# Moving the key shift, the second scan's output and the score visits in a hybrid block kernel on one Trainium2 core

## What is computed

```python
h = rmsnorm(x, norm_w);  p = h @ w_in
r, k, v, g, dw, da = split(token_shift(pa, mu))        # branch 1
kk = k * k_k;  kh = kk / max(norm_per_head(kk), 1e-12)
def step(s, inp):                                       # per head, 64 x 64 state
    sa = einsum('bhvk,bhk->bhv', s, kh_t)
    s = s * w_t - sa[..., None] * b_t + v_t[..., None] * k_t
    return s, einsum('bhvk,bhk->bhv', s, r_t)
oa = (layer_norm_per_head(y) * ln_w + ln_b + bonus) * silu(g)
ob = rmsnorm((ssd_chunked(silu(conv4(xbc))) + d_skip * xs) * silu(z))   # branch 2
oc = bg * conv3(cg * xin) * silu(g3)                                    # branch 3
merged = sum_n sigmoid(gate_n) * (o_n @ w_branch[n]);  out = rmsnorm(x + merged @ w_out)
```

## Time and profile before

| | |
|---|---|
| median of 3 runs (lowest, highest) | 1231.09 us (1230.35, 1233.09) |
| profiled execution: its time, its span | 1228.37 us, 1226.7 us |
| mean granted TensorE clock | 0.989 |
| TensorE matmuls busy | 1179.1 us, 96% |
| VectorE busy | 803.7 us, 66% |
| ScalarE busy | 574.2 us, 47% |
| GpSimd busy | 69.9 us, 6% |
| HBM traffic over the span | 160 GB/s |

### The profile page before, as it was taken

The page is one execution under the profiler, slowest core; times in us unless marked ns, Lnnn a source line. Parts: engine busy times, 40 slices in busy tenths (PEclk is TensorE's granted clock), DMA queues, the critical chain, the costliest instruction groups (busy, mean ns, idle before and its releaser), DMA issues.

```text
span 1226.7 us, 23555 instructions
## 1 busy us (share of the span) xinstructions
PE 1179.1 (96%) x8502; PEld 1047.3 (85%) x8502; DVE 803.7 (66%) x1174; ACT 574.2 (47%) x828; POOL 69.9 (6%) x94
## 2 busy tenths in 40 slices
PE   6998999999999999999999999999999999999996
PEld 5997989989889899899898988888888888888885
DVE  4786768688577686876867857564555555546553
ACT  5454445454354463544444544544444344444443
POOL 2001001010010010100101003000000000000000
PEclk9998999999999999999999999999999999999998
DMA  5755645546455354463553545566666656667662
GB/s 165 207 155 137 165 119 138 140 113 162 125 137 150 103 154 133 136 163 109 138 150 103 140 148 171 172 206 193 195 191 197 193 190 193 193 188 273 199 192 98
DMA packets 254747, 197.24 MB, mean 161 GB/s; under 512 B 23943, under 2 KB 207472, under 8 KB 254064
## 3 DMA queue, kind: packets, MB, share of 16 engines
q1 hardware_dynamic: 252228, 195.82, 55.0%
q10 hardware_dynamic: 2476, 0.84, 0.3%
HBM read 193.71 MB, written 2.11 MB: 160 GB/s over the span
## 4 chain that ended last, share of the span: by engine, by line
PE 91%; DVE 4%; ACT 1%; DMA 1%; issue 1%; POOL 1%; DVEq 0%; SPq 0%; ACTq 0%
PE ps L1158 14%; PE ps L1159 13%; PE ps L1160 13%; PE ps L1236 11%; PE ps L1237 11%; PE ps L1238 11%; PE ps L1484 2%; PE ps L1485 2%; PE ps L1486 2%; DVE wlo L721 1%; DVE lots L1040 1%; PE ps L1270 1%; ACT whi L427 1%; PE ps L1353 1%; PE ps L1345 1%
## 5 line engine op out<-in xcount | busy, mean ns | idle before, releaser
L721 DVE TENSOR_TENSOR wlo<-raw,whi 128x1024 fp32r<-128x1024 f32 (+1 forms) x356 | 439.8, 1247 | 239.4 <-ACT whi L427 237.9
L427 ACT ACTIVATE whi<-raw 128x1024 fp32r<-128x1024 f32 (+1 forms) x356 | 373.4, 1054 | 316.8 <-PE ps L1238 181.2
L1158 PE MATMUL ps<-hhi,whi 128*128 128x256 f32 (+1 forms) x1440 | 424.9, 295 | 0.2 <-DVE wlo L721 0.2
L1159 PE MATMUL ps<-hlo,whi 128*128 128x256 f32 (+1 forms) x1440 | 409.8, 285 | 0.0
L1160 PE MATMUL ps<-hhi,wlo 128*128 128x256 f32 (+1 forms) x1440 | 409.4, 284 | 0.0
L1158 PEld LDWEIGHTS ps<-hhi,whi 128*128 128x128 f32 (+1 forms) x1440 | 276.9, 192 | 17.3 <-issue 13.8
L1159 PEld LDWEIGHTS ps<-hlo,whi 128*128 128x128 f32 (+1 forms) x1440 | 277.4, 193 | 0.7
L1160 PEld LDWEIGHTS ps<-hhi,wlo 128*128 128x128 f32 (+1 forms) x1440 | 276.9, 192 | 0.3
L1236 PE MATMUL ps<-whi,hhi 128*128 128x512 f32 x384 | 151.3, 394 | 0.0
L1238 PE MATMUL ps<-whi,hlo 128*128 128x512 f32 x384 | 149.6, 390 | 0.0
L1237 PE MATMUL ps<-wlo,hhi 128*128 128x512 f32 x384 | 149.5, 389 | 0.0
(11 more groups left out here) (270 smaller groups left out, 1140.6 us busy)
## 6 DMA issues: line engine op xcount, KB each, us to landing
raw<-in_w_in SPq DMA_DIRECT2D x548, 256.0 KB, 3.1
raw<-in_w_branch SPq DMA_DIRECT2D x96, 256.0 KB, 3.6
raw<-in_w_out SPq DMA_DIRECT2D x64, 256.0 KB, 3.6
o<-in_x SPq DMA_DIRECT2D x4, 1024.0 KB, 6.7
acb<-acs_rows SPq DMA_DIRECT2D x8, 256.0 KB, 3.5
out_y<-lots SPq DMA_DIRECT2D x3, 512.0 KB, 4.6
lots<-in_final_norm_w SPq DMA_DIRECT2D x1, 1024.0 KB, 10.3
lots<-ad SPq DMA_DIRECT2D x32, 8.0 KB
```

The lines of the kernel that those rows point to most:

```text
L427: sc.activation(whi[:, slot, :, 0:width], raw[:, slot, :, 0:width], ACT.Copy).then_inc(hi_done, 1)
L721: tt(wlo[:, slot, :, 0:width], raw[:, slot, :, 0:width], whi[:, slot, :, 0:width].bitcast(F32), ALU.subtract).then_inc(lo_done, 1)
L1158: mm(dst, a, khi, start=first, stop=False)
L1159: mm(dst, a, klo, start=False, stop=False)
```

## The change

Three groups of moves. In the scheme of slots, `V_P1` goes from 17 to 16, and with it everything that is counted from it; `V_XT` and `V_YB` go to 18 and 20, in front of the transition matrices, and their matmuls write bank C in place of E; the convolution and its tanh go with them (visits 14 and 16), and the masked inverse is made at visit 15. TensorE gets one more wait before the transition matrices, for the reader of bank C. Scores and transposes go one slot ahead on TensorE (3, 5, 7 to 2, 4, 6) and on the other engines (4, 6 to 3, 5; the copy at visit 9 to 7); the DMAs of the inverse that ScalarE sends go from visit 15 to 14, while the inverse itself stays at visits 9 to 12. On VectorE the layer norm is cut in two: reciprocal and first product, then `shift_rk` of the next round, then the last three operations at visit 33. The low splits at two visits of the scan go behind the state operations. The queue of SyncE is not edited.

```diff
 ORDER = (1, 0, 2, 3)
-V_P1 = 17
-V_XT = 25
-V_YB = 27
+V_P1 = 16
+V_XT = 18
+V_YB = 20
...
 
+            def shift_tile(j, a, t, bank, strip):
...
+                w = ORDER[2 * a + t]
+                proj(strip, t, bank + t, pq[:, w, 1:1 + T])
+                sc.activation(qq[:, w, :], ps[:, bank + t, 0:T], ACT.Copy,
+                              scale=omm[:, bass.ds(j + w * CT, 1)]).then_inc(tile_out, 1)
...
             def shift_pair(j, a, bank, strip):
...
                 for t in range(2):
-                    w = ORDER[2 * a + t]
-                    proj(strip, t, bank + t, pq[:, w, 1:1 + T])
-                    sc.activation(qq[:, w, :], ps[:, bank + t, 0:T], ACT.Copy,
-                                  scale=omm[:, bass.ds(j + w * CT, 1)]).then_inc(tile_out, 1)
+                    shift_tile(j, a, t, bank, strip)
...
                         sc.activation(s2g, sh[:, 3, :], ACT.Tanh, scale=0.5).then_inc(s["g_th"], 1)
-                    if t == 4:
+                    if t == 3:
...
                         sc.activation(seg, seg, ACT.Exp, scale=-1.0).then_inc(s["seg_e"], 1)
-                    if t == 9:
+                    if t == 7:
...
                         act.wait_ge(s["x_tr2"], j + 1)
-                        sc.activation(xst.rearrange("p b n -> p (b n)"), E[:, 0:T], ACT.Copy,
+                        sc.activation(xst.rearrange("p b n -> p (b n)"), C[:, 0:T], ACT.Copy,
...
                         proj(strip0 + 1, 1, BANKS[1] + 1, scb[:, 1, :]).then_inc(tile_out, 1)
-                    if t == 15:
+                    if t == 14:
...
                             act.dma_start(tb[:, q, :, :], sol_2[8 * q:8 * q + 8, :, :, :]).then_inc(s["t_in"], 16)
+                    if t == 16:
+                        act.wait_ge(s["x_s"], j * 4 + 4)
+                        sc.activation(cvt, cv, ACT.Tanh, scale=0.5).then_inc(s["x_th"], 1)
...
                         sc.activation(yy, A, ACT.Copy).then_inc(s["yx_ok"], 1)
-                        act.wait_ge(s["x_s"], j * 4 + 4)
-                        sc.activation(cvt, cv, ACT.Tanh, scale=0.5).then_inc(s["x_th"], 1)
...
                         sc.activation(yz.rearrange("p q n -> p (q n)"), A, ACT.Copy).then_inc(s["yz_ok"], 1)
-                    if t == 32:
+                    if t == 29:
...
                         sc.activation(ys, B[:, 0:T], ACT.Copy).then_inc(s["ys_ok"], 1)
-                    if t == 32 and not last:
-                        shift_pair(j + 1, 0, BANKS[3], strip0 + 3)
+                    if t in (31, 32) and not last:
+                        shift_tile(j + 1, 0, t - 31, BANKS[3], strip0 + 3)
...
                 for t in range(2 * (LAST + GATES) if last else SLOTS):
-                    if t % 2 == 0 and t // 2 < nchunks and t != V_ST + 2:
+                    if t % 2 == 0 and t // 2 < nchunks and t not in (V_ST + 1, V_ST + 3):
...
                         stt(s2g, s2g, 1.0, sh[:, 3, :], ALU.add, ALU.mult)
-                    if t == 4:
+                    if t == 3:
                         scores(0)
-                    if t == 6:
+                    if t == 5:
                         scores(1)
-                    if t == 17:
+                    if t == V_P1 - 1:
...
                         op.then_inc(s["state_ok"], 1)
-                    if t == V_ST + 2 and t // 2 < nchunks:
+                    if t in (V_ST + 1, V_ST + 3) and t // 2 < nchunks:
                         split_lo(base + t // 2 + AHEAD, (t // 2 + AHEAD) % RING)
-                    if t == 33:
+                    if t == 30:
...
                         v.tensor_copy(sol_l, sol_t.rearrange("p s t -> p t s")).then_inc(s["sol_tr"], 1)
-                    if t == 19:
+                    if t == 14:
...
                         conv4(s["x_s"], j * 4, j)
-                    if t == 21:
+                    if t == V_P1 + 3:
...
                         seg_times(1, 1).then_inc(s["seg_g"], 1)
-                    if t == 22:
+                    if t == V_XT - 1:
...
                         dve.wait_ge(s["yb_mm"], j + 1)
-                        stt(cv, xs2, dskh[:, bass.ds(j, 1)], E[:, T:2 * T], ALU.mult, ALU.add).then_inc(s["ob_d"], 1)
+                        stt(cv, xs2, dskh[:, bass.ds(j, 1)], C[:, T:2 * T], ALU.mult, ALU.add).then_inc(s["ob_d"], 1)
...
                         stt(yc, C[:, 0:T], -1.0 / 64, ys, ALU.mult, ALU.add).then_inc(s["yc_ok"], 1)
-                    if t == 29:
+                    if t == 27:
...
                             op.then_inc(s["sc_s"], 1)
-                    if t == 30:
+                    if t == 28:
...
                         tt(yo, yc, rin, ALU.mult).then_inc(s["ln_v"], 1)
+                    if t == 32 and not last:
+                        shift_rk(j + 1)
+                    if t == 33:
...
                             ).then_inc(s["oa_ok"], 1)
-                    if t == 33 and not last:
-                        shift_rk(j + 1)
...
                         norm_and_logits(j + 1)
-                    if t == 3:
+                    if t == 2:
...
                         op.then_inc(s["tr_vk"], 1)
-                    if t == 5:
+                    if t == 4:
...
                         score(1)
-                    if t == 7:
+                    if t == 6:
...
 
+                        pe.wait_ge(s["ob_d"], j + 1)
...
                         pe.wait_ge(s["xs_ok"], j + 1)
-                        pe.wait_ge(s["nm_ok"], j * 2 + 2)
+                        pe.wait_ge(s["vt_ok"], j + 1)
                         for b in range(2):
-                            op = tr(E[:, b * P:b * P + P], xs2[:, b * P:b * P + P], ident[:])
+                            op = tr(C[:, b * P:b * P + P], xs2[:, b * P:b * P + P], ident[:])
...
                             h = slice(64 * e, 64 * e + 64)
-                            mm(E[h, T:2 * T], xst[:, 0, h], seg[:, e, 0:T], start=True, stop=False, skip_group_check=True)
-                            op = mm(E[h, T + P:2 * T], xst[:, 1, h], seg[:, e, T:384], start=False, stop=True,
+                            mm(C[h, T:2 * T], xst[:, 0, h], seg[:, e, 0:T], start=True, stop=False, skip_group_check=True)
+                            op = mm(C[h, T + P:2 * T], xst[:, 1, h], seg[:, e, T:384], start=False, stop=True,
```

## The result

| | before | after |
|---|---|---|
| median (lowest, highest), 4 runs each | 1230.72 (1228.54, 1233.09) | 1250.17 (1249.10, 1251.49) |
| profiled execution, its span | 1228.37, 1226.7 | 1250.56, 1248.8 |
| mean granted clock | 0.989 | 0.983 |

The ratio is 1.0158, with a 95% interval of 1.0137 to 1.0180, so the loss is 19.5 us where 9.4 were forecast. The direction was right. The median lies just above the top of the stated range, 1250.0, and the size was off by a factor of two. The two profiled executions lie 22.2 us apart, since that of the kernel before is 2.4 us under its median. Lines behind the edits have new numbers in the code after: 1207, 1287 and 1315 are 1212, 1292 and 1320 there, 945 is 949, 721 is 725.

The account below looks back on a forecast made before the run. Bound by TensorE's matmuls with one hole a round: new losses 24.4 + 2.4 + 1.4 + 7 x 0.1 + 6.5 = 35.4 less 26.0 won gave +9.4 on 1231.1, so 1240.5 us. Its own range was 1234 to 1249, the overall one 1225 to 1250.

Parts of the forecast that it names:

- new wait for the inverse: TensorE at line 1315 waits for the masked inverse, 3.05 us in each of eight rounds: 24.4 us lost.
- hole at the turn: TensorE's wait at the key norm, line 1207, between rounds shrinks from 2.9 to 0.1 us in seven rounds.
- wait for the scaled keys: TensorE at line 1287 waits 0.35 us in seven rounds, 2.4 us, plus 1.4 us in the first round.
- clock, by the length of rounds: Half clock at the turns goes, winning 5.7 us; half clock behind the waits at line 1315 costs 6.5 us.
- Clock behind the new waits: Half clock follows the waits at line 1315 at the turns' rate: 8 x 4/7 x 1.42 = 6.5 us, bounds 0 and 11.4.
- rival of a solve that SyncE doesn't hold: Diagonals go out once reduced, ScalarE alone holds the solve: wait 1.95 us at line 1315, time 1224.5; chance 0.17.
- a turn with 1.4 us: Wait of 1.4 us stays between rounds because ScalarE reaches the sqrt late: 9.8 us more, 1250; chance 0.13.

Follow-up runs that it names:

- e3_sp: Changed kernel with both halves of the score diagonals sent ahead of chunk 9's load in SyncE's queue: 1235.64 us, 1.0046 of the kernel before.
- e4_scores: Changed kernel with scores and transposes back at their old slots and visits, the rest of the change kept: 1215.52 us, 0.9873 of the kernel before.
- e5_conv: Changed kernel with the four convolution taps at visit 15, behind the masked inverse instead of ahead of it: 1249.44 us, 1.0148 of the kernel before.
- e9_scores_only: Kernel before with only the transposes and scores moved one slot ahead, with their visits on VectorE and ScalarE: 1256.68 us, 1.0188 of the kernel before.
- e7_turn: Changed kernel with scores at the old slots and the key shift behind the whole layer norm again: 1234.42 us, 1.0033 of the kernel before.
- e8_best: Changed kernel with scores at old slots, diagonals ahead of chunk 9's load, and the short convolution's high part behind the sqrt: 1203.22 us, 0.9778 of before.
- e6_pad: Changed kernel with the two transposes of line 1427 made five times over, 0.9 us more TensorE work a round: 1252.27 us.
- e2_before: The kernel before, run once more without any edit, for the clock: 1228.96 us.

## Why the prediction was wrong in size

Point by point, by its own steps, in the profiled executions:

| step | forecast | measured |
|---|---|---|
| new wait for the inverse, eight rounds | +24.4 | +22.2 |
| hole at the turn | -20.3 + 0.7 | -16.1 |
| wait for the scaled keys | +3.8 | +5.0 |
| clock, by the length of rounds | -5.7 + 6.5 = +0.8 | -5.7 + 12.5 = +6.8 |
| matmuls busy for longer, not assigned | none | +4.3 |
| sum | +9.4 | +22.2 (the span: +22.1) |

- **The new wait** was right in place, cause and size. e3_sp shows SyncE's share, e4_scores that the moved scores and transposes bring it, e5_conv that taps and DMAs end together; e9_scores_only brings the wait forth in the old kernel.
- **The turn** was right in mechanism. The forecast 0.1 was 0.59, since the product of line 1039 took 0.4 us longer beside GpSimd's. The prediction didn't see that the new order lays it there. e7_turn prices the moved shift. e8_best closes the hole though that product is as long as before: its copy, load and low half are out of the way, and the load is over 1.36 us before the sqrt.
- **The scaled keys:** 0.35 forecast, 0.41 measured, in each of seven rounds. The first round's was 2.5 in this execution and 1.7 in the other; the forecast 1.4 came on top of the 0.3 that it had before.
- **The step that failed is "Clock behind the new waits".** It took the rate of the turns, 4 of 7, at 1.42 us each: 6.5 us. Measured: 8 of 8, one of them double, 12.5 us by the length of rounds. The price of 1.42 held; the rate didn't, and the prediction had no double stretches. That term was mis-sized by 6.0 us, the largest part of the 12.7 between forecast and measured span; the 4.3 that are not assigned and the turn's 3.5 come next. Its stated bound, 11.4 for eight of eight, came near, but the sum went by the rate. I took the rate of one execution for a chance per hole. e6_pad shows nearly equal holes met three times, spared four times and met once more, and e2_before other turns in the same kernel, so a rate counted in one execution is neither a property of the hole nor safely carried to another schedule. That this rate came from an execution 2.4 us under the median makes it a low one besides.

The loss between the medians is 2.7 us less than between the profiled executions. The prediction added its forecast for the fast profiled execution to the median. The kernel before's executions near the median have mean clocks of 0.985 to 0.988, the profiled one 0.989, so the median most likely holds more lost clock than 4 of 7, and part of the clock's error doesn't show in the medians.

The rival of a solve that SyncE doesn't hold was refuted, the one of a turn with 1.4 us too: ScalarE does reach the sqrt late, but for the load's 1.28 alone. The figure that the Trainium skill gives for the drain of a table switch (ScalarE: Activation LUTs, What ACT_TABLE_LOAD costs) is contradicted here by ScalarE's rows after the change, where split, load and sqrt start at 347.19, 348.25 and 349.54, each as the one before ends.

What stays open: what sets the falls of the clock, and with it why the holes of the middle met half clock eight times of eight and those of the turns four of seven. e6_pad rules out the place alone; which distances are bad no run has measured. The 4.3 us of longer matmuls are open too.

## What to carry to other kernels

When a visit is moved past a split in an in-order queue, follow what the split releases: here a load in SyncE's queue, and behind it a small DMA on which the next solve hung. In a matmul-bound kernel, price a recurring hole with its clock, from none to all of the holes, and let the range hold both ends: holes of 2.5 to 3.6 us in one kernel met stretches that lack from 0 to 3.4 us (e6_pad). Don't take the count from one execution. Take a hole away altogether rather than shift it: in e8_best, whose longest hole in the rounds is 0.9 us, the loss of clock was gone too.

## What the runs showed of the hardware that was not expected

- Half clock at holes of 2.5 to 3.4 us at one place came 24 times of 24 in three executions (the changed kernel's two and e5_conv), and 4 times of 8 in one execution where each round had 0.9 us more work. Holes of 1.6 to 1.7 us met it twice in seven (e3_sp), those of 1.6 to 2.3 us four times in eight (e9_scores_only), and 2.2 us five times in seven (e7_turn). At waits of 0.2 to 0.97 us (e4_scores, e8_best) it never came.
- A stretch of half clock in the rounds lacked either 1.7 or 3.4 us by the windows, nothing between, and made its round about 1.4 or 2.6 us longer. All twelve double stretches in the rounds of these executions began 0.2 to 1.6 us before TensorE started again. All single ones began between 0.1 us ahead of that start and 1.8 us behind it.
- Beside a GpSimd product a VectorE split took 1.67 to 1.68 us in seven rounds, where the splits of the same execution with no GpSimd operation beside them took 1.20 to 1.23, and the product of line 1039 took 0.83 to 0.84 in place of 0.42.
